# Expert rows streamed from HBM: earlier banks, a choice cut into pieces, scores two groups behind, single rows at the end

## The chip, the cores and the metric

The kernel runs on one core of one Trainium2 chip. The metric is the device time of one execution in microseconds (us), lower is better; three executions of the kernel before gave 1175.29, 1179.24 and 1180.07 us.

## The reference, cut to what matters

Two transformer blocks work on 256 tokens of 1024 features. The first has two recurrent mixers and a gated feed-forward layer. The second has retention, stick-breaking attention, an output projection and at its end PEER, a mixture over 16384 experts of one neuron each. For each token and each of 8 heads, PEER scores two lists of 128 sub-keys, takes the 16 best of each list, adds all 16 x 16 pairs, takes the 16 best pairs, and so has 128 experts per token. It then reads a row of `expert_down` and one of `expert_up` for each:

```
top_s, top_i = lax.top_k(sub_scores, K)
cand_s = top_s[:, :, 0, :, None] + top_s[:, :, 1, None, :]
best_s, best_c = lax.top_k(cand_s.reshape(T, PEER_HEADS, K * K), K)
gate = jax.nn.softmax(best_s, axis=-1)
a = jnp.einsum('pd,ped->pe', xb, expert_down[ib])
act = jax.nn.gelu(a, approximate=False) * gb
y = jnp.einsum('pe,ped->pd', act, expert_up[ib])
```

Here K is 16, and the last three lines run for 128 tokens at a time.

## The kernel before, in words

All of it is one program with an instruction order written by hand for each engine; engines meet through counting semaphores. Up to the last 700 us it multiplies with weights that stream through a ring of slots (16 in `ring_sb`, 6 in `whi`, 4 in `x_rows`).

PEER works on **columns**. Column `col` (0 to 255) is one chosen expert for each of 128 tokens; columns 0 to 127 belong to tokens 0 to 127 (tile 0), the rest to tile 1. Head h of a tile is choice n = 8 * tile + h and gives columns 16n to 16n + 15. For each column:

- POOL issues one indirect DMA (L2062) that gathers 128 rows of 8 KB, 1 MB in all, into a row buffer. It needs the expert numbers of the choice (`VTI`) and a free buffer.
- DVE takes the dot product of the first half of each row with its token (L2006).
- For a group of columns (`GR`) ACT then takes the Gelu (L1353), DVE multiplies by the gates (L2011), and ACT makes a diagonal matrix for each column (L1358).
- PE multiplies the second half of the rows with the diagonal (L905 and L908, in `add_rows`) and adds it up in PSUM. After that the buffer is free.

There are 16 row buffers of 8 KB in the end, but at first only 7: the others still hold query weights `w_q`. POOL takes buffers from a first-in, first-out list (`free`). When PE has used the weights of head h, their buffer enters the list, at the place that `after` gives: behind column 3 for head 0, 7 for head 1, 11 for head 2, 19 for head 3, 27, 43, 59 and 75 for heads 4 to 7. So column 7 uses the buffer of column 0, column 10 that of column 3, column 11 that of head 0, column 16 that of head 1, column 21 that of head 2, and column 26 that of column 16.

Around the columns the same engines still do this. PE computes queries by head (`query_tile` for one tile, L846, for heads 0 to 2; `query_half` for both tiles, L860, from head 3 on), then ACT copies the query, PE computes the scores of the two lists (`scores`, L872), ACT copies them. DVE makes a choice n (`choose`: two lists, the pairs, the decoding into expert numbers, the gates). The dicts `second_at`, `query_at` and `choose_at` say at which group i of the main loop each runs. Choices 0 and 1 run before the loop. Tile 1 also needs its part of the output projection (`second_out`), its residual (`second_gate`, `second_add` at L1908), the sums of squares (`second_sums`, L925), the root (`n3_root`, L1290 and L1292) and the norm (`second_norm`, `shifted`).

Functions of ACT need tables: Gelu one, Exp and Ln others; a change of table is an ACT_TABLE_LOAD.

In front of PEER stands the output projection of tile 0 (`out_half`, L810). Each pair of its output blocks has a PSUM bank of a ring of four, and `bank()` makes PE wait until the bank's last reader is done. All four waits stand ahead of the first product:

```
outs = [bank((VN, ("wo2", 2 * i + 1, 0))) for i in range(4)]
```

The bank used second is read last by the gate's product at L1875 on DVE. Then follow the norm of tile 0, the queries and scores of heads 0 and 1, choice 0, and the first gather.

## Time and profile before

| what | value |
|---|---|
| executions | 1175.29, 1179.24, 1180.07 us, median 1179.24 |
| profiled execution | 1178.07 us, its span 1176.3 us |
| PE busy | 1030.6 us (88%), 5156 matmuls |
| DVE busy | 855.7 us (73%) |
| ACT busy | 419.9 us (36%) |
| gathers by POOL | 256, 268.45 MB, 55.3% of 16 DMA engines' span |
| HBM read | 376.61 MB |
| mean granted clock of TensorE | 0.956 |
| chain that ended last | PE 45%, DMA 31%, DVE 15%, ACT 5% |

Busy shares are averages over stages with different limits. The span begins with the first instruction; 1.8 us of the execution lie around it.

### The profile page before, as it was taken

The page shows a single profiled execution, that of the slowest core. Times are in us where ns is not written, and L with a number is a line of the kernel's source. Part 1 is how long each engine was busy: PE and PEld are TensorE (multiplying, and loading weights), DVE is VectorE, ACT ScalarE, POOL GpSimd, SP SyncE. Part 2 cuts the span into 40 slices and gives each one's busy share as a digit, 9 for nine tenths or more (in the row PEclk, how much of TensorE's full clock was granted, in tenths as well). Part 3 has the DMA queues.
Part 4 walks back from the last instruction along what each step waited for, and adds up shares of the span by engine and source line. Part 5 has one row for each costly group of instructions (what it writes and reads, how often), then busy time and mean ns, then how long its engine had stood idle before and what let it go on. Part 6 is the DMA issues. An engine that isn't in the chain of part 4 may idle for free.

```text
span 1176.3 us, 14387 instructions
## 1 busy us (share of the span) xinstructions
PE 1030.6 (88%) x5156; PEld 721.4 (61%) x5156; DVE 855.7 (73%) x1780; ACT 419.9 (36%) x833; POOL 285.8 (24%) x260
## 2 busy tenths in 40 slices
PE   6999999999999999988899998888668767887878
PEld 6988999999998876874555544333323323332433
DVE  5977689998868993384778767766786677677554
ACT  5644544445456654233223222221221222222112
POOL 0000000000000000034445543454335434443520
PEclk9999999999999999989999998898899889888998
DMA  9532449979927433479999999999999999999994
GB/s 357 204 125 90 147 180 350 354 293 322 326 89 309 139 109 124 180 284 340 364 420 422 422 421 421 422 420 421 423 422 421 422 422 419 423 421 421 422 421 183
DMA packets 67896, 378.61 MB, mean 322 GB/s; under 512 B 7537, under 2 KB 7921, under 8 KB 35057
## 3 DMA queue, kind: packets, MB, share of 16 engines
q0 software_dynamic: 36864, 268.45, 55.3%
q1 hardware_dynamic: 29808, 106.09, 25.0%
q10 hardware_dynamic: 1152, 3.15, 0.8%
q8 instruction: 42, 0.69, 0.2%
q14 instruction: 30, 0.24, 0.1%
HBM read 376.61 MB, written 1.05 MB: 321 GB/s over the span
## 4 chain that ended last, share of the span: by engine, by line
PE 45%; DMA 31%; DVE 15%; ACT 5%; issue 4%; POOL 1%; SPq 0%; DVEq 0%; ACTq 0%
DMA whi_rows<-in_peer,idsb 26%; PE pb L905 7%; PE pb L428 7%; PE pb L425 7%; PE pb L908 6%; PE pb L453 4%; DMA ring_sb<-in_peer,idsb 3%; DVE ring_lo L1417 3%; PE pb L640 2%; PE pb L810 2%; PE pb L860 1%; DVE ring_sb L2006 1%; PE pb L470 1%; PE pb L472 1%; PE pb L471 1%
## 5 line engine op out<-in xcount | busy, mean ns | idle before, releaser
L2006 DVE CUSTOM_DVE_ANT_0 ring_sb<-ring_sb,arena 128x1024 f32<-128x1024 f32 x137 | 166.9, 1225 | 106.8 <-DMA ring_sb<-in_peer,idsb 106.8
L905 PE MATMUL pb<-ring_sb,arena 128*128 128x512 f32 x274 | 154.2, 646 | 98.8 <-ACT arena L1358 98.7
L2062 POOL DMA_INDIRECT ring_sb<-in_peer,idsb x137 | 150.4, 1098 | 237.0 <-PE pb L908 210.2
L425 PE MATMUL pb<-xhi,whi 128*128 128x256 f32 x736 | 190.9, 293 | 1.1 <-ACT xhi L986 0.5
L428 PE MATMUL pb<-xlo,whi 128*128 128x256 f32 x736 | 186.3, 287 | 0.5 <-DVE xlo L1636 0.3
L2062 POOL DMA_INDIRECT arena<-in_peer,idsb x38 | 41.4, 1090 | 546.2 <-DVE idsb L1984 503.4
L1353 ACT ACTIVATE arena<-arena 128x4 f32<-128x4 f32 (+2 forms) x71 | 14.6, 205 | 400.4 <-DVE arena L2006 400.4
L1417 DVE TENSOR_TENSOR ring_lo<-ring_sb,whi 128x1024 fp32r<-128x1024 f32 x126 | 147.6, 1218 | 13.4 <-ACT whi L959 13.3
L905 PEld LDWEIGHTS pb<-ring_sb,arena 128*128 128x128 f32 x274 | 52.3, 202 | 167.9 <-issue 167.4
L908 PE MATMUL pb<-ring_sb,arena 128*128 128x512 f32 x274 | 151.0, 634 | 0.0
L425 PEld LDWEIGHTS pb<-xhi,whi 128*128 128x128 f32 x736 | 142.5, 194 | 5.4 <-issue 3.4
L428 PEld LDWEIGHTS pb<-xlo,whi 128*128 128x128 f32 x736 | 142.6, 194 | 4.5 <-issue 2.7
L959 ACT ACTIVATE whi<-ring_sb 128x1024 fp32r<-128x1024 f32 x126 | 125.4, 1047 | 12.5 <-DMA ring_sb<-in_w_down 9.0
L908 PEld LDWEIGHTS pb<-ring_sb,arena 128*128 128x128 f32 x274 | 55.9, 204 | 72.8 <-issue 72.8
L1358 ACT ACTIVATE arena<-cs,arena 128x128 f32<-128x128 f32 x256 | 82.6, 390 | 16.3 <-DVE arena L2011 15.6
L453 PE MATMUL pb<-xhi,ring_lo 128*128 128x256 f32 x546 | 78.6, 284 | 0.0
L2006 DVE CUSTOM_DVE_ANT_0 whi_rows<-whi_rows,arena 128x1024 f32<-128x1024 f32 x40 | 49.0, 1226 | 34.6 <-DMA whi_rows<-in_peer,idsb 34.6
L453 PEld LDWEIGHTS pb<-xhi,ring_lo 128*128 128x128 f32 x546 | 71.6, 193 | 0.0
L2006 DVE CUSTOM_DVE_ANT_0 arena<-arena 128x1024 f32<-128x1024 f32 x38 | 46.4, 1224 | 13.5 <-DMA arena<-in_peer,idsb 13.5
L2062 POOL DMA_INDIRECT whi_rows<-in_peer,idsb x40 | 46.6, 1165 | 38.7 <-PE pb L908 29.2
L1682 DVE SCALAR_TENSOR_TENSOR arena<-ring_sb,small,arena 128x1024 f32<-128x1024 f32 x42 | 51.9, 1278 | 0.0
L425 PE MATMUL pb<-ahi,whi 128*128 128x256 f32 x176 | 49.9, 284 | 0.0
(356 smaller groups left out, 1783.8 us busy)
## 6 DMA issues: line engine op xcount, KB each, us to landing
ring_sb<-in_ada SPq DMA_DIRECT2D x48, 512.0 KB, 5.6
ring_sb<-in_w_gu SPq DMA_DIRECT2D x44, 512.0 KB, 6.9
ring_sb<-in_w_in SPq DMA_DIRECT2D x38, 512.0 KB, 8.3
ring_sb<-in_w_down SPq DMA_DIRECT2D x22, 512.0 KB, 5.9
ring_sb<-in_w_out SPq DMA_DIRECT2D x16, 512.0 KB, 3.6
ring_sb<-in_w_q SPq DMA_DIRECT2D x8, 512.0 KB, 3.6
whi_rows<-in_w_q SPq DMA_DIRECT2D x6, 512.0 KB, 7.5
ring_sb<-in_peer,idsb POOLq DMA_INDIRECT x137, 27.7
```

Source lines behind the costliest of these rows:

```text
L425: e.matmul(o, hi_w(u)[:, c], xh(k), start=start, stop=False, skip_group_check=skip)
L428: e.matmul(o, hi_w(u)[:, c], xl(k), start=False, stop=False, skip_group_check=skip)
L453: e.matmul(o, lo_w(u)[:, kc(k)], hi_of(k), start=False, stop=False)
L640: mm = e.matmul(o, lo_w(u)[:, kc(n)], ah_of(k), start=False, stop=False, skip_group_check=True)
L905: mm = e.matmul(pb[4 + 2 * tile][:, :], dgr[col % 8], o[:, 1024:1536], start=begin, stop=end)
L908: e.matmul(pb[5 + 2 * tile][:, :], dgr[col % 8], o[:, 1536:2048], start=begin, stop=end).then_inc(*PU.up(("row", col)))
L959: e.activation(hi_w(u), slot(u), ACT.Copy).then_inc(*HI.up(u))
L1358: e.activation(dgr[col % 8], c_("ident"), ACT.Copy, scale=ae[:, col:col + 1]).then_inc(*AD.up(("dg", col)))
L1417: e.tensor_tensor(lo_w(u), slot(u), hi_w(u).bitcast(F32), SUB).then_inc(*LOV.up(u))
L1682: e.scalar_tensor_tensor(out=o, in0=slot(u), scalar=cs8[:, k:k + 1], in1=o, op0=MUL, op1=ADD).then_inc(*VM.up(("ada", n)))
L2006: e.tensor_tensor_reduce(o, o, h2t[tile], 1.0, 0.0, MUL, ADD, aa[:, col:col + 1]).then_inc(*VD.up(("dot", col)))
L2062: e.indirect_dma_start(rows_at[s], None, peer, bass.IndirectOffsetOnAxis(ap=idsb[:, col:col + 1], axis=0)).then_inc(s_row[s], 16)
```

## The change

First, the banks of the output projection are awaited one by one, in the order 0, 2, 3, 1 of the ring. Second, choice 1 is cut into pieces (`best_of_list`, `pair_up`, `best_of_pairs`, `decode`, `gates`), and the dots of columns 0 to 3 and their weights stand between the pieces. ACT runs the Exp of choice 1 behind group 1 and the root of tile 1 ahead of group 2. Third, the query of head 2, tile 0 moves behind the first group on PE. A query of the loop now stands behind `add_rows` in its group, and the scores of that query two groups later (on ACT: the copy of the query one group later and of the scores three). The `second_at` entry of head 2 moves from group 5 to 9, queries of later heads one group earlier, choices from 3 on one group later. `after` reads GR[i - 1] for GR[i - 2]: buffers of heads 0, 1, 2 enter the list behind columns 7, 11 and 31, those of heads 3 to 7 behind 19, 27, 43, 59 and 75 as before. Fourth, columns 240 to 255 are two groups of two and twelve of one, where they were two of four and eight of one.

```
-        GR = [range(0, 2), range(2, 4)] + [range(i, i + 4) for i in range(4, 248, 4)] + [range(i, i + 1) for i in range(248, 256)]
+        GR = [range(0, 2), range(2, 4)] + [range(i, i + 4) for i in range(4, 240, 4)] + [range(i, i + 2) for i in range(240, 244, 2)] + [range(i, i + 1) for i in range(244, 256)]
-        second_at = {3: 0, 4: 1, 5: 2}
-        query_at = {6: (3, 0), 7: (3, 1)} | {4 * h - 8 + j: (h, j) for h in range(4, 8) for j in range(2)}
-        choose_at = {4: 2, 8: 3} | {4 * n - 6: n for n in range(4, 16)}
+        second_at = {3: 0, 4: 1, 9: 2}
+        query_at = {5: (3, 0), 6: (3, 1)} | {4 * h - 9 + j: (h, j) for h in range(4, 8) for j in range(2)}
+        choose_at = {4: 2, 9: 3} | {4 * n - 5: n for n in range(4, 16)}
...
-            outs = [bank((VN, ("wo2", 2 * i + 1, 0))) for i in range(4)]
-            where["wo2"] = outs
+            outs = where["wo2"] = [(turn[0] + i) % 4 for i in (0, 2, 3, 1)]
+            turn[0] += 4
             for i in range(4):
+                bank((VN, ("wo2", 2 * i + 1, 0)), outs[i])
                 out_half(0, i, range(4, 8), pb[outs[i]])
...
-            query_tile(2, 0)
...
             for i in range(NB + 1):
-                if i in second_at:
-                    query_tile(second_at[i], 1)
-                if i in query_at:
-                    query_half(*query_at[i])
                 if i == 60:
                     keep_clock(10)
                 if i:
                     add_rows(i - 1)
                 if i == 1:
+                    query_tile(2, 0)
+                if i == 2:
                     second_sums()
                     scores(2, (0,))
+                if i - 2 in second_at:
+                    scores(second_at[i - 2], (1,))
+                if i - 2 in query_at and query_at[i - 2][1]:
+                    scores(query_at[i - 2][0], (0, 1))
                 if i in second_at:
-                    scores(second_at[i], (1,))
-                if i in query_at and query_at[i][1]:
-                    scores(query_at[i][0], (0, 1))
+                    query_tile(second_at[i], 1)
+                if i in query_at:
+                    query_half(*query_at[i])
...
             choose(0)
             second_gate(range(4))
-            choose(1)
-            second_gate(range(4, 8))
             for i in range(NB + 1):
-                if i - 1 in query_at and query_at[i - 1][1]:
-                    scores(query_at[i - 1][0], (0, 1))
-                if i - 1 in second_at:
-                    scores(second_at[i - 1], (1,))
+                if i == 2:
+                    n3_root(1)
                 if i < NB:
                     prepare(i)
                 if i == 0:
+                    second_gate(range(4, 8))
+                if i == 1:
+                    choose(1)
                     query_tile(2, 0)
                     second_squares()
-                if i == 1:
-                    n3_root(1)
+                if i == 2:
                     scores(2, (0,))
-                if i == 2:
                     shifted(1)
-                if i in second_at:
-                    query_tile(second_at[i], 1)
-                if i in query_at and query_at[i][1]:
-                    query(query_at[i][0])
+                if i - 3 in second_at:
+                    scores(second_at[i - 3], (1,))
+                if i - 3 in query_at and query_at[i - 3][1]:
+                    scores(query_at[i - 3][0], (0, 1))
+                if i - 1 in second_at:
+                    query_tile(second_at[i - 1], 1)
+                if i - 1 in query_at and query_at[i - 1][1]:
+                    query(query_at[i - 1][0])
...
             choose(0)
-            choose(1)
-            for i in range(NB + 1):
+            best_of_list(1, 0)
+            dot(0)
+            best_of_list(1, 1)
+            dot(1)
+            pair_up(1)
+            weigh(0)
+            best_of_pairs(1)
+            dot(2)
+            dot(3)
+            decode(1, 0, 16)
+            weigh(1)
+            second_add()
+            gates(1)
+            for i in range(2, NB + 1):
                 if i < NB:
                     prepare(i)
-                if i == 0:
-                    second_add()
...
-            after = {GR[i - 2][-1]: h for i, h in second_at.items()} | {GR[i - 2][-1]: h for i, (h, j) in query_at.items() if j}
+            after = {GR[i - 1][-1]: h for i, h in second_at.items()} | {GR[i - 1][-1]: h for i, (h, j) in query_at.items() if j}
```

## Rows read from the trace of the kernel before

**Rows 1.** Page, part 2: GB/s moved by the DMA engines, 40 slices of 29.4 us.

```profile
GB/s 357 204 125 90 147 180 350 354 293 322 326 89 309 139 109 124 180 284 340 364 420 422 422 421 421 422 420 421 423 422 421 422 422 419 423 421 421 422 421 183
```

**Rows 2.** Busy time by stretch (PE, PEld, DVE, ACT, POOL, PEclk, DMA share, GB/s).

```profile
1000.00:1010.00 10.00, 8.49 (x13) 3.66 (x14) 6.73 (x14) 2.97 (x10) 2.60 (x2) 0.63 1.01 421
...
1160.00:1165.00 5.00, 5.00 (x13) 2.23 (x12) 2.86 (x7) 1.21 (x4) 0.00 (x0) 1.00 0.06 26
```

**Rows 3.** Timeline, DVE: dots of rows 11, 26, 28 and 255 (start us, us, operation, idle, releaser).

```profile
544.08 1.23 DVE L2006 CUSTOM_DVE_ANT_0 ring_sb<-ring_sb,arena 128x1024 f32<-128x1024 f32 x1 [3.06 <-DMA ring_sb<-in_peer,idsb]
...
587.09 1.23 DVE L2006 CUSTOM_DVE_ANT_0 ring_sb<-ring_sb,arena 128x1024 f32<-128x1024 f32 x1 [3.32 <-DMA ring_sb<-in_peer,idsb]
...
592.97 1.22 DVE L2006 CUSTOM_DVE_ANT_0 x_rows<-x_rows,arena 128x1024 f32<-128x1024 f32 x1 [0.81 <-DMA x_rows<-in_peer,idsb]
...
1166.57 1.23 DVE L2006 CUSTOM_DVE_ANT_0 x_rows<-x_rows,arena 128x1024 f32<-128x1024 f32 x1 [0.80 <-DMA x_rows<-in_peer,idsb]
```

**Rows 4.** Timeline, POOL: gathers 0, 7, 11, 24 and 26 issued.

```profile
503.82 1.08 POOL L2062 DMA_INDIRECT arena<-in_peer,idsb  x1 [503.37 <-DVE idsb L1984]
...
524.42 1.20 POOL L2062 DMA_INDIRECT arena<-in_peer,idsb  x1 [10.30 <-PE pb L908]
...
538.59 0.94 POOL L2062 DMA_INDIRECT ring_sb<-in_peer,idsb  x1 [3.98 <-PE pb L846]
...
569.19 1.99 POOL L2062 DMA_INDIRECT ring_sb<-in_peer,idsb  x1 [0.30 <-issue]
...
581.48 0.94 POOL L2062 DMA_INDIRECT ring_sb<-in_peer,idsb  x1 [9.06 <-PE pb L908]
```

**Rows 5.** Timeline, PE: end of the last projection, then the second block's output projection.

```profile
470.46 0.28 PE L454 MATMUL pb<-xhi,ring_lo 128*128 128x256 f32 x1
473.01 1.24 PE L810 MATMUL pb<-xn,ring_sb 128*128 128x128 f32 x9 [2.27 <-DVE arena L1875]
```

**Rows 6.** Timeline, DVE: the second choice, and the residual addition of tile 1.

```profile
507.49 0.29 DVE L1917 MAX8 arena<-arena 128x8 f32<-128x128 f32 x1
...
511.45 0.43 DVE L1917 MAX8 arena<-arena 128x8 f32<-128x256 f32 x1
...
513.82 0.15 DVE L1949 TENSOR_SCALAR arena<-arena 128x1 f32<-128x1 f32 x1
...
516.56 0.17 DVE L1984 SCALAR_TENSOR_TENSOR idsb<-arena 128x16 uint32<-128x16 f32 x1
...
519.73 1.22 DVE L1908 TENSOR_TENSOR hT<-hT,arena 128x1024 f32<-128x1024 f32 x1
```

**Rows 7.** Timeline, PE: query tile, first row, scores of tile 1, half a query.

```profile
512.75 3.74 PE L846 MATMUL pb<-xn,ring_sb 128*128 128x128 f32 x32
...
520.39 2.05 PE L905 MATMUL pb<-arena 128*128 128x512 f32 x2 [3.91 <-ACT arena L1358]
...
573.68 1.05 PE L872 MATMUL pb<-subk_sb,sq 128*128 128x128 f32 x4 [3.41 <-ACT sq L1324]
...
586.19 3.62 PE L860 MATMUL pb<-xn,ring_sb 128*128 128x256 f32 x16
```

**Rows 8.** Timeline, ACT: root of tile 1's norm, then the table for the Gelu.

```profile
528.69 0.37 ACT L1290 ACTIVATE stdt<-pb,cs 128x128 f32<-128x128 f32 x1 [3.00 <-PE pb L925]
...
530.97 1.28 ACT L1353 ACT_TABLE_LOAD   x1
```

**Rows 9.** Timeline, PE and ACT: three groups near the end, last diagonal, last row.

```profile
1138.09 1.10 PE L905 MATMUL pb<-ring_sb,arena 128*128 128x512 f32 x2 [2.85 <-ACT arena L1358]
...
1148.05 2.04 PE L905 MATMUL pb<-ring_sb,arena 128*128 128x512 f32 x2 [2.85 <-ACT arena L1358]
...
1168.27 0.40 ACT L1358 ACTIVATE arena<-cs,arena 128x128 f32<-128x128 f32 x1 [0.23 <-DVE arena L2011]
...
1168.29 1.02 PE L905 MATMUL pb<-whi_rows,arena 128*128 128x512 f32 x2
...
1170.01 1.02 PE L905 MATMUL pb<-x_rows,arena 128*128 128x512 f32 x2
```

More of the change, by code:

```diff
@@ L1995, in choose, with dot, weigh @@
                 gates(n)
-            def prepare(i):
-                for col in GR[i]:
-                    tile = col // 128
-                    s, v = row_of[col]
-                    o = rows_at[s][:, 0:1024]
-                    e.wait_ge(s_row[s], v)
-                    if col % 128 == 0:
-                        for g in range(2):
-                            e.wait_ge(*AQ.at((("h2t", tile), g)))
-                    e.tensor_tensor_reduce(o, o, h2t[tile], 1.0, 0.0, MUL, ADD,
-                                           aa[:, col:col + 1]).then_inc(*VD.up(("dot", col)))
+            def dot(col):
+                tile = col // 128
+                s, v = row_of[col]
+                o = rows_at[s][:, 0:1024]
+                e.wait_ge(s_row[s], v)
+                if col % 128 == 0:
+                    for g in range(2):
+                        e.wait_ge(*AQ.at((("h2t", tile), g)))
+                e.tensor_tensor_reduce(o, o, h2t[tile], 1.0, 0.0, MUL, ADD, aa[:, col:col + 1]).then_inc(*VD.up(("dot", col)))
+            def weigh(i):
                 cols = slice(GR[i].start, GR[i].stop)
@@ L2011, in prepare @@
                 e.tensor_tensor(ae[:, cols], ae[:, cols], gts[:, cols], MUL).then_inc(*VD.up(("act", i)))
+            def prepare(i):
+                for col in GR[i]:
+                    dot(col)
+                weigh(i)
                 if i in choose_at:
```

48 lines of the change are left out of this document (29 added, 19 removed).

## The prediction

> **What bounds the kernel now.** I read the page's DMA lines first. From the slice at 588 us to the last but one the engines move 419 to 423 GB/s, and before that, from the first gather on, less [rows 1]. A steady stretch gives 421 GB/s [rows 2], so a gather of 1.049 MB takes 2.49 us. From there on nothing but the DMA sets the pace. What can be won is the time that the DMA lost before, and what follows the last landing.
>
> So I list when rows landed, by the dots that waited for them. Row 11 landed at 544.08, row 26 at 587.09, row 28 at 592.97, the last, 255, at 1166.57 [rows 3]. From row 28 there are 227 gathers in 573.6 us, 2.53 each: the queue is never empty again. **The end is the landing of row 28 plus a constant plus the tail.** Gather 0 is issued at 503.82, gather 7 at 524.42, gather 11 at 538.59, gather 26 at 581.48 [rows 4]. Gathers 11 and 26 met an empty queue: they landed 5.5 and 5.6 us after their issue. Row 28 would, at 2.49 us a row and 5.6 us for the first, have landed at 503.8 + 5.6 + 28 x 2.49 = 579.1; it landed 13.9 us later. That is all that better feeding can give.
>
> Near the end only a sixteenth of the rate is left (26 GB/s from 1160 on, [rows 2]) while rows still land, the last at 1166.57: one engine of the 16 is behind the others and sets the end. It has the same bytes to move after the change.
>
> **The change part by part.**
>
> Banks. PE ends the last projection at 470.74 and starts the output projection at 473.01, after 2.27 us of idling on the gate's product on DVE [rows 5]. Awaited one by one with that bank last, three pairs of blocks (5.4 us of products) go ahead of it. I take 2.2 us, and all before gather 0 is one chain, so gather 0 goes from 503.8 to 501.6. Bounds: 0 if another bank is late too, 2.27.
>
> Choice 1 in pieces. Before, DVE ran it in one, from 507.49 to 517.0, and only then the dots of rows landed long ago [rows 6]. A list costs 1.7, pairing 0.55, the pairs' best 2.5 (511.45 to 513.97), decoding 2.8 (to 516.73) [rows 6], a dot 1.15 to 1.2 [rows 3]. In the new order from 505.3: list to 507.0; dot 0 waits for row 0 (501.6 + 5.6 to 6) and ends at 508.8; list 510.5; dot 1 511.7; pairing and weights 512.5; pairs 515.1; dots 2 and 3 517.4; decoding 520.3; weights 520.5; the addition of 1.2 (519.73, [rows 6]) to 521.7. PE gets its first row at 513.1 where it was 520.39 [rows 7], a gain of 7.3; the buffers of rows 0 and 1 are free at 515 and 517. Gathers 7 and 8 now queue behind gather 6 (landing at 522 or later: 501.6 + 5.6 + 6 x 2.49), so the hole in front of 524.42 [rows 4] closes. The expert numbers of choice 1 come at 520.3 instead of 516.7; that is covered, since gather 16 needs a buffer that comes far later. If the cover were gone it would cost 3.6.
>
> What is late next is group 2, columns 4 to 7. Its dots can run from 524 on, but on ACT the root of tile 1 now stands ahead of its Gelu. Chain: weights of group 1 at 520.5, two diagonals to 521.3, a table load of 1.28 (as the one in [rows 8]), Exp to 523.1, copy and squares to 524.5. PE has added rows 2 and 3 by then (521.2 to 524.7, 1.72 each by two rows of [rows 9]; query tile 2 with its 3.74 us [rows 7] lies ahead, from 516.7 to 520.4, in a gap). Sums take 1.9, to 526.6. From the root's start to the Gelu of the group there were 532.25 - 528.69 = 3.6 us, of which a 0.4 copy is now behind [rows 8]: Gelu at 530.0, PE at row 4 at 531.0. So gather 11, which now takes row 4's buffer, is issued at 533.1 and lands at 538.7. **Gain at row 11: 5.4 us.**
>
> What the trace shows of a table load is 1.28 us of ACT [rows 8], and the change has one more of them on this chain. The Trainium skill (ScalarE: Activation LUTs, What ACT_TABLE_LOAD costs) gives 2.66 us for a switch, with the drain. That would make this sum 1.4 us worse; the chain as traced (Ln, load, Exp, copy, load, Gelu in 3.6 us) has no room for it, so the row decides.
>
> Scores two groups behind. At 573.68 PE waited 3.41 us for ACT's copy of a query, which stood behind the group's dots, and then did the scores and half a query before the rows of that group [rows 7]; gather 26 waited 9.06 us for them [rows 4], and the queue ran dry. In the new order PE takes the rows first. By 2.49 us a row from row 11: row 15 lands at 548.8, its group is weighed at 550.5, choice 2 (9.5 us as choice 1) ends at 560.2, rows 16 to 19 are ready for PE at 565.7, gather 25 is issued at 567.9 and lands at 573.5, where the queue would have it at 573.6. So this spot closes, just. Queries and scores stay on PE (3.6 us for half a query, [rows 7]) between groups and are covered while each group's period is 9.95.
>
> From row 11 to row 28 took 48.9 us; 17 gathers at 2.49 are 42.3. Of the 6.6 over, 2.1 is the hole at row 26. The other 4.5 came with the queue not empty, but shallow. I take that 2.0 of them go with a fuller queue and 2.5 stay (bounds 0 and 4.5). **Gain from 11 to 28: 4.1.**
>
> Clock. PE has nothing between 527.2 and 531.0. After 3.91 us of idling the clock was at its lower level, 1.2 GHz, for the first rows: two matmuls took 2.05 us [rows 7]. After 2.85 they took 2.04 once and 1.10 once [rows 9], and after 2.27 it stayed high [rows 5]. If it falls, rows 4 and 5 take 1.7 us longer, gather 11 with them. I put 1.3 for it.
>
> Fewer buffers. Columns 12 to 43 have one less in flight (head 0's buffer enters four columns later, head 1's too, head 2's twenty later). It costs nothing as long as the spots above close; uncovered it is 2.49 us at each.
>
> Tail. Before, the group of four at 1148.05 met half clock, and PE then had no pause until the end: the last diagonal was there at 1168.67, PE came to it at 1170.01 [rows 9]. With single columns from 244 on (1.72 of each 2.49 us) it starts on the diagonal: 1.2 us. Bounds: 0, and a loss of 1.7 if the clock is at half for the last column.
>
> Sum: 5.4 + 4.1 - 1.3 + 1.2 = 9.4 us. The profiled execution is 1178.1 (span 1176.3 and 1.8 around it), so 1168.7; the median of the runs is 1.2 above it. I say 1169.5.
>
> **The rivals.**
>
> A, the DMA's own pace. All 4.5 us stay, the clock falls, the tail gives half: 5.4 + 2.1 - 1.7 + 0.6 = 6.4, about 1172.5. For it: rows 12 to 24 came in over 2.49 each with gathers queued.
>
> B, the holes move. One buffer less makes gathers 15 and 25 late, both of which I find with no slack. Two holes of 2.49 and the clock leave 9.4 - 5.4 = 4, about 1175: no change that can be measured. Against it: rows first on PE.
>
> C, slower. Gather 11 waits for the root on ACT. If its chain is 3 us longer than I have it, gather 11 gains 2.4 and not 5.4, and each of choices 2, 3 and 4, with nine to eleven buffers in flight, then opens a hole of 4 us. Together 9.4 - 3 - 12 = -5.6: about 1184. It decides from the point where gather 25 is issued after 577.
>
> D, dots against gathers. While dots ran without a pause an issue took 1.99 us, where it took 0.94 at 538.59 [rows 4]; now dots run while gathers 3 to 6 are issued. At most 4 us on POOL, and four gathers queue ahead of them, so the time is that of the forecast, or 1 us more. The Trainium skill (SBUF — State Buffer, SBUF: two separate sides) has GpSimd locked out of writing descriptors while a DVE operation holds the port pair that both share; by it alone the first gathers come late.
>
> E, the change does more: all 4.5 go, the clock holds: 1165.
>
> **How the numbers follow.** Forecast with D 0.56, own range 1166 to 1171.5; A 0.17, B 0.16, C 0.04, E 0.07. A measurement here can tell about 0.5%, 5.9 us, from no change, so under 1173.3 is faster. Faster: 0.56 + 0.14 of A + 0.07 = 0.77; same: 0.03 of A + 0.16 = 0.19; slower 0.04. The range leaves out C, half of E and the worse half of B: 1165 to 1175.5.
>
> **What would show it.** Output projection at 470.9 and gather 0 at 501.6; PE's first row at 513; gather 7 before 517; gather 11 at 533 and its row at 539; no wait of POOL over 6 us on rows 16 to 19; row 28 at 584 to 585; the last landing 8 us earlier; PE on the last row right behind its diagonal. It is wrong if row 11 lands after 542, or if rows 11 to 28 take 48 us or more.

## The result and the profile after

The changed kernel takes 1169.01 us (median of 4 runs, 1167.22 to 1170.07), the kernel before on the same chip 1178.9 (4 runs). The ratio is 0.992, 95% interval 0.9893 to 0.9946. The profiled execution took 1169.98 us, with a span of 1168.1. It is faster by 0.8%, clear of noise, and the forecast was 1169.5. Two executions that lie far out, 2063.16 us of the kernel with a hole in mid-stream and 1691.88 us of the kernel before, both in a slow state, stand in no figure below.

The spans differ by 8.2 us. The timelines say where they went, in stretches that follow one another:

| stretch | before | after | gained |
|---|---|---|---|
| start to gather 0 issued | 503.82 | 500.48 | 3.3 |
| gather 0 to row 11 landed | 40.26 | 38.43 | 1.8 |
| row 11 to row 28 | 48.89 | 47.38 | 1.5 |
| row 28 to row 255 | 573.60 | 573.22 | 0.4 |
| row 255 to the end | 9.7 | 8.6 | 1.1 |

The page's line of the DMA rate for the kernel after, 40 slices of 29.2 us, for [rows 1]:

```profile
GB/s 358 207 126 91 148 178 358 349 291 320 325 105 289 162 108 117 191 330 341 364 423 421 421 422 421 421 422 421 421 421 421 422 422 421 422 421 422 421 421 198
```

The bound is what it was: 421 to 423 GB/s from 584 us on. The slice from 496 to 526 us moved 330 GB/s where 284 stood, the two behind it 341 and 364, where 340 and 364 stood.

The timeline of DVE after, the dots that answer to [rows 3] (rows 11, 25 to 28 and 255; columns as there):

```profile
538.91 1.23 DVE L2022 CUSTOM_DVE_ANT_0 ring_sb<-ring_sb,arena 128x1024 f32<-128x1024 f32 x1 [5.58 <-DMA ring_sb<-in_peer,idsb]
...
577.03 1.22 DVE L2022 CUSTOM_DVE_ANT_0 arena<-arena 128x1024 f32<-128x1024 f32 x1 [3.15 <-DMA arena<-in_peer,idsb]
579.84 1.23 DVE L2022 CUSTOM_DVE_ANT_0 x_rows<-x_rows,arena 128x1024 f32<-128x1024 f32 x1 [1.57 <-DMA x_rows<-in_peer,idsb]
583.09 1.23 DVE L2022 CUSTOM_DVE_ANT_0 ring_sb<-ring_sb,arena 128x1024 f32<-128x1024 f32 x1 [2.02 <-DMA ring_sb<-in_peer,idsb]
586.29 1.23 DVE L2022 CUSTOM_DVE_ANT_0 ring_sb<-ring_sb,arena 128x1024 f32<-128x1024 f32 x1 [1.54 <-DMA ring_sb<-in_peer,idsb]
...
1159.51 1.23 DVE L2022 CUSTOM_DVE_ANT_0 ring_sb<-ring_sb,arena 128x1024 f32<-128x1024 f32 x1 [0.80 <-DMA ring_sb<-in_peer,idsb]
```

Row 28 lands 6.7 us earlier than in [rows 3] and row 255 7.1. Row 25 came 4.38 us behind row 24 (572.65), where a full queue gives 2.49: there is still a hole, one row ahead of the old one.

The timeline of POOL after, gathers 0, 4, 7, 9, 11 and 25, for [rows 4]:

```profile
500.48 1.07 POOL L2094 DMA_INDIRECT arena<-in_peer,idsb  x1 [500.04 <-DVE idsb L2001]
...
506.27 1.98 POOL L2094 DMA_INDIRECT ring_sb<-in_peer,idsb  x1 [0.85 <-PE pb L810]
...
513.46 1.62 POOL L2094 DMA_INDIRECT arena<-in_peer,idsb  x1 [2.50 <-PE pb L909]
...
521.06 0.94 POOL L2094 DMA_INDIRECT x_rows<-in_peer,idsb  x1 [4.45 <-PE pb L909]
...
532.29 1.85 POOL L2094 DMA_INDIRECT ring_sb<-in_peer,idsb  x1 [8.02 <-PE pb L909]
...
571.07 1.17 POOL L2094 DMA_INDIRECT arena<-in_peer,idsb  x1 [10.07 <-PE pb L909]
```

The wait of 10.30 us in front of gather 7 is down to 2.50, as the pieces were meant to do. But POOL then waits 8.02 us in front of gather 11 and 10.07 in front of gather 25. The waits moved more than they shrank.

The timeline of PE after, for [rows 5], [rows 7] and [rows 9]: the last projection and the output projection, the first row, row 4, the rows of group 5, the last row.

```profile
469.62 0.28 PE L454 MATMUL pb<-xhi,ring_lo 128*128 128x256 f32 x1
469.74 2.51 PE L810 MATMUL pb<-xn,ring_sb 128*128 128x128 f32 x21
...
511.23 1.10 PE L906 MATMUL pb<-arena 128*128 128x512 f32 x2 [1.66 <-ACT arena L1362]
...
528.61 2.05 PE L906 MATMUL pb<-ring_sb,arena 128*128 128x512 f32 x2 [3.87 <-ACT arena L1362]
...
567.04 2.05 PE L906 MATMUL pb<-arena 128*128 128x512 f32 x2 [3.52 <-ACT arena L1362]
568.88 1.92 PE L909 MATMUL pb<-arena 128*128 128x512 f32 x2
570.58 1.92 PE L906 MATMUL pb<-x_rows,arena 128*128 128x512 f32 x2
...
1161.76 1.10 PE L906 MATMUL pb<-ring_sb,arena 128*128 128x512 f32 x2 [0.51 <-ACT arena L1362]
```

The reader is to see three things. The 2.27 us of idling in front of the output projection is gone. The first row comes at 511.23, 9.2 us earlier than in [rows 7]. And twice PE idled over 3.5 us and then worked at the lower clock, 1.2 GHz: two matmuls in 2.05 us, where at 2.4 GHz they take 1.02. The second of these falls on group 5, and gather 25 waits for the buffer of that group's first row.

The timeline of ACT after, for [rows 8], the root of tile 1 and its two table loads, then the Gelu of group 2:

```profile
524.33 0.37 ACT L1292 ACTIVATE stdt<-pb,cs 128x128 f32<-128x128 f32 x1 [1.12 <-PE pb L925]
524.71 1.28 ACT L1294 ACT_TABLE_LOAD   x1
526.00 0.31 ACT L1294 ACTIVATE rstd<-stdt 128x128 f32<-128x128 f32 x1
526.33 1.28 ACT L1357 ACT_TABLE_LOAD   x1
527.62 0.20 ACT L1357 ACTIVATE arena<-arena 128x4 f32<-128x4 f32 x1
```

Group 2's rows had been multiplied on DVE by 526; their Gelu waits for the root ahead of it. Row 4 on PE waits for the Gelu, and gather 11 for row 4's buffer.

### The profile page after: what moved, and what is told of

Read it like the earlier page. It is cut to its first block, busy times and chain, and to the rows that moved or that the text cites. A ratio compares the mean times of both kernels' runs of the same rounds, so it can differ in the third digit from the quotient of the medians.

```text
span 1168.1 us, 14405 instructions
## 1 busy us (share of the span) xinstructions
PE 1032.5 (88%) x5156; PEld 720.9 (62%) x5156; DVE 854.8 (73%) x1784; ACT 421.3 (36%) x838; POOL 290.2 (25%) x260
## 4 chain that ended last, share of the span: by engine, by line
PE 46%; DMA 30%; DVE 15%; ACT 5%; issue 4%; POOL 1%; SPq 0%; POOLq 0%; DVEq 0%; ACTq 0%
DMA xn<-in_peer,idsb 22%; PE pb L906 8%; PE pb L428 7%; PE pb L425 7%; PE pb L909 7%; DMA ring_sb<-in_peer,idsb 5%; PE pb L453 4%; DVE ring_lo L1422 3%; PE pb L640 2%; PE pb L810 2%; PE pb L861 1%; DVE ring_sb L2022 1%; DMA arena<-in_peer,idsb 1%; PE pb L470 1%; PE pb L472 1%
## 5 line engine op out<-in xcount | busy, mean ns | idle before, releaser
L906 PE MATMUL pb<-ring_sb,arena 128*128 128x512 f32 x274 | 152.1, 639 | 73.7 <-ACT arena L1362 73.7
L2094 POOL DMA_INDIRECT ring_sb<-in_peer,idsb x137 | 162.2, 1184 | 193.8 <-PE pb L909 175.7
L2022 DVE CUSTOM_DVE_ANT_0 ring_sb<-ring_sb,arena 128x1024 f32<-128x1024 f32 x137 | 164.3, 1223 | 53.5 <-DMA ring_sb<-in_peer,idsb 53.5
L2094 POOL DMA_INDIRECT arena<-in_peer,idsb x38 | 39.9, 1049 | 567.9 <-DVE idsb L2001 500.0
L1422 DVE TENSOR_TENSOR ring_lo<-ring_sb,whi 128x1024 fp32r<-128x1024 f32 x126 | 147.5, 1220 | 13.3 <-ACT whi L961 13.3
L909 PE MATMUL pb<-ring_sb,arena 128*128 128x512 f32 x274 | 148.3, 624 | 0.0
L2022 DVE CUSTOM_DVE_ANT_0 arena<-arena 128x1024 f32<-128x1024 f32 x38 | 46.5, 1224 | 31.8 <-DMA arena<-in_peer,idsb 31.8
L906 PE MATMUL pb<-arena 128*128 128x512 f32 x76 | 43.2, 652 | 27.7 <-ACT arena L1362 27.6
L2022 DVE CUSTOM_DVE_ANT_0 x_rows<-x_rows,arena 128x1024 f32<-128x1024 f32 x30 | 36.7, 1224 | 31.9 <-DMA x_rows<-in_peer,idsb 31.9
```

The source lines that it names most:

```text
L906: mm = e.matmul(pb[4 + 2 * tile][:, :], dgr[col % 8], o[:, 1024:1536], start=begin, stop=end)
L909: e.matmul(pb[5 + 2 * tile][:, :], dgr[col % 8], o[:, 1536:2048], start=begin, stop=end).then_inc(*PU.up(("row", col)))
L1422: e.tensor_tensor(lo_w(u), slot(u), hi_w(u).bitcast(F32), SUB).then_inc(*LOV.up(u))
L2022: e.tensor_tensor_reduce(o, o, h2t[tile], 1.0, 0.0, MUL, ADD, aa[:, col:col + 1]).then_inc(*VD.up(("dot", col)))
L2094: e.indirect_dma_start(rows_at[s], None, peer, bass.IndirectOffsetOnAxis(ap=idsb[:, col:col + 1], axis=0)).then_inc(s_row[s], 16)
```

## The experiments

All ratios are against the kernel before, timed on the same chip in the same rounds. The kernel after was not timed again beside them, so an experiment is compared with it by ratio (0.992, interval 0.9893 to 0.9946) and by landings counted from gather 0, one trace each. How far such landings differ by chance can be seen from the kernels before, banks alone and tail alone, which have the same order between gather 0 and row 28: there row 28 lands 89.15, 89.82 and 89.15 us behind gather 0, row 255 662.75, 662.47 and 661.76. So 1 us at row 255 says nothing, and 2 us not much.

**The banks alone** (the kernel before, with this edit):

```diff
-            outs = [bank((VN, ("wo2", 2 * i + 1, 0))) for i in range(4)]
-            where["wo2"] = outs
+            outs = where["wo2"] = [(turn[0] + i) % 4 for i in (0, 2, 3, 1)]
+            turn[0] += 4
             for i in range(4):
+                bank((VN, ("wo2", 2 * i + 1, 0)), outs[i])
```

> The kernel before with the banks awaited one by one, nothing else. Theory (everything ahead of gather 0 is one chain, and the holes behind it keep their size): gather 0 and all landings 2.3 us earlier, time 2.3 us less than the kernel before (ratio 0.998). Rival (the holes in the queue at rows 7 to 26 are tied to engines that are late for other reasons and absorb it): gather 0 is 2.3 us earlier, row 28 under 1 us earlier, no gain in time.

1174.2 us, ratio 0.997 [0.9955, 0.9985]. Gather 0 at 500.41 and the last row at 1162.88, 662.5 behind it (662.8 before): the gain before gather 0 goes through to the end whole. Of the 3.4 us in this trace 0.9 lie ahead of the edit, where this execution ran earlier (the last projection ends at 469.83, before at 470.74), so 2.5 are the banks'. The time is 3.7 us less where 2.3 was expected.

**The tail alone** (the kernel before, with the last sixteen columns as two twos and twelve singles):

> The kernel before with the last sixteen columns as two twos and twelve singles. Theory (PE's backlog after a group of four at the lower clock is what the end waited for): from the landing of row 255 to the end of the span 8.6 us instead of 9.7, time 1.1 us less (0.999). Rival (only the clock counts, and it falls at another place): PE still has no pause in the last 15 us, and the distance from last landing to end stays at 9.7.

1176.95 us, ratio 0.9993 [0.9977, 1.001], as a time not to be told from nothing. In the trace the last row lands at 1165.46 and the span ends at 1174.0, 8.5 us later, where it was 9.7 before. That is what the theory expected, and yet it does not show that the edit did it: the kernel with the banks alone and the one with rows and list alone (below) end on the old groups of columns, and there too it is 8.5 and 8.6 us. PE near the end of the kernel with the banks alone, a group of four and the last row:

```profile
1144.34 2.05 PE L906 MATMUL pb<-ring_sb,arena 128*128 128x512 f32 x2 [2.83 <-ACT arena L1359]
...
1165.12 1.10 PE L906 MATMUL pb<-x_rows,arena 128*128 128x512 f32 x2 [0.23 <-ACT arena L1359]
```

The lower clock met this group of four too, but for two pairs of matmuls (2.05 and 1.54 us) and not for four (2.04, 1.91, 1.91 and 1.43 us in the trace of before), and PE had caught up before the last row. In the kernel with rows and list alone every pair from 1136.7 us on takes 1.02 to 1.10 us. So the 9.7 us are those of one trace in three with the old groups; what the edit is worth on the average is not shown.

**No pieces** (the kernel after, with choice 1 in one stretch, the root and `query_tile(2, 0)` where they were before):

```diff
-            best_of_list(1, 0)
-            dot(0)
-            best_of_list(1, 1)
-            dot(1)
...
+            choose(1)
+            for i in range(NB + 1):
```

> The changed kernel with choice 1 in one piece ahead of the dots again, and root, query tile 2 and residual back where they were; banks, scores two behind and tail stay. Theory (the pieces are what brings gather 11 forward by some 3 us beyond the banks): the hole in front of gather 7 is back, gather 7 issued near 521, row 11 lands near 541 to 542, time 3 us over the changed kernel, about 1172. Rival (the slots of heads 0 and 1, entering the list later, are what holds gather 11): row 11 as in the changed kernel at 539, time within 1 us of it.

1169.51 us, ratio 0.9925 [0.9901, 0.9949]: the same time as the kernel after. That is the rival's figure; the theory had 1172. The timeline of POOL, gathers 6, 7 and 11:

```profile
509.49 0.94 POOL L2082 DMA_INDIRECT ring_sb<-in_peer,idsb  x1 [0.85 <-PE pb L810]
520.57 1.34 POOL L2082 DMA_INDIRECT arena<-in_peer,idsb  x1 [10.14 <-PE pb L909]
...
531.01 0.94 POOL L2082 DMA_INDIRECT ring_sb<-in_peer,idsb  x1 [2.12 <-PE pb L909]
```

The old wait in front of gather 7 is back, 10.14 us, and yet row 11 lands at 539.30, only 0.4 us later than with pieces. What both kernels have alike is PE's row 4: 528.61 with pieces, 528.78 without. It hangs on the Gelu of group 2, and for that Gelu two things are due at almost the same time. One is the root of tile 1 with its table loads, which the pieces do not shorten: with them it ends at 527.62, without them at 527.39. The other is the dot of row 7, which the pieces make earlier. Without them it comes last:

```profile
526.54 1.23 DVE L2020 CUSTOM_DVE_ANT_0 arena<-arena 128x1024 f32<-128x1024 f32 x1 [3.13 <-DMA arena<-in_peer,idsb]
527.80 0.20 ACT L1356 ACTIVATE arena<-arena 128x4 f32<-128x4 f32 x1 [0.41 <-DVE arena L2020]
```

So the pieces take away one bound and meet the other 0.2 us ahead of it. They issue gathers 7 to 10 5 to 7 us earlier; the queue works them off and then stands empty in front of gather 11. Busy time where the queue ran dry (columns as in [rows 2]), first without pieces, then with them:

```profile
520.00:523.00 3.00, 3.00 (x16) 1.91 (x15) 3.00 (x5) 1.98 (x3) 1.55 (x2) 1.00 0.32 60
```

```profile
530.00:535.00 5.00, 5.00 (x11) 2.13 (x10) 2.69 (x6) 2.68 (x7) 2.40 (x2) 0.85 0.12 30
```

An early stretch was bought with a hole of much the same size four rows later. The pieces also brought the fall of the clock at row 4: without them PE idles 1.10 us there and a pair takes 1.10 us.

**No scores** (the kernel after, with queries, scores, choices and the list of buffers where they were before; banks, pieces and tail stay):

> The changed kernel with scores, queries, choices and the entry of the buffers back where they were; banks, pieces and tail stay. Theory (scores two behind spare PE the wait for ACT's copy in front of group 5, and the hole at row 25 or 26): PE idles over 3 us for the copy of a query again, the hole at row 26 is at least as deep as before (4.5 us or more between landings) and row 28 lands 1 to 3 us later than in the changed kernel; time 1170 to 1172. Rival (fewer buffers in flight cost as much as the order gives): row 28 within 1 us, time equal to the changed kernel or below it.

1175.85 us, ratio 0.9982 [0.9968, 0.9996]. Gather 26 waits 9.07 us at 580.74, as in [rows 4], and row 28 lands at 592.58, 6.3 us later than in the kernel after. The theory had the direction, but 1 to 3 us for row 28 and 1170 to 1172 for the time: this part is worth more than it said. Banks and pieces together land row 28 91.6 us behind gather 0, the banks alone 89.8, and the time is 1.65 us above that of the banks alone in the same rounds: without the other part the pieces bring nothing and by the trace cost 1.8 us.

**Rows and list alone.** What is left of the gain is in the third part. This kernel is the one before with two edits of it:

```diff
             for i in range(NB + 1):
-                if i in second_at:
-                    query_tile(second_at[i], 1)
-                if i in query_at:
-                    query_half(*query_at[i])
                 if i == 60:
                     keep_clock(10)
                 if i:
                     add_rows(i - 1)
+                if i in second_at:
+                    query_tile(second_at[i], 1)
+                if i in query_at:
+                    query_half(*query_at[i])
...
-            after = {GR[i - 2][-1]: h for i, h in second_at.items()} | {GR[i - 2][-1]: h for i, (h, j) in query_at.items() if j}
+            after = {GR[i - 1][-1]: h for i, h in second_at.items()} | {GR[i - 1][-1]: h for i, (h, j) in query_at.items() if j}
```

> The kernel before, with two things of the change: add_rows stands ahead of the query products on TensorE, and the list of buffers follows (GR[i - 1]). Scores stay in the group of their query product, banks, pieces and tail as before. Counted from gather 0's issue, row 28 landed after 89.2 us before and after 85.8 us in the kernel after. Theory (rows first is most of the gain, the scores two groups behind the smaller part): row 28 86.5 us behind gather 0, time 1174 to 1175.5 us. Rival (TensorE's wait for ScalarE's copy of the query is the cost, so that the scores' place is what brings the gain): row 28 89 us behind gather 0, time 1177.5 us.

1172.08 us, ratio 0.995 [0.9931, 0.9969]. Row 28 lands 84.2 us behind gather 0 (89.2 before, 85.8 after), row 255 656.7 (662.8 before, 659.0 after). So by row 28 these two edits bring 5.0 us, where the whole change brings 3.3 behind gather 0. Another 1.1 comes behind row 28, but the kernels with the banks alone and the tail alone are 1.0 us shorter there too, so it can't be put down to these edits. POOL's gathers 25 and 26 show the gain; no wait is over 3 us where one of 9.06 was:

```profile
570.20 1.47 POOL L2062 DMA_INDIRECT ring_sb<-in_peer,idsb  x1 [1.25 <-PE pb L846]
574.13 0.94 POOL L2062 DMA_INDIRECT arena<-in_peer,idsb  x1 [2.45 <-PE pb L908]
```

Theory expected 86.5 and left something for the scores' new place; rival 89. Neither left room for what came.

**The old list under the new order** (the kernel after, with the line of `after` alone taken back):

> The kernel after, with the one line of the buffer list as before: a buffer that a head's query weights held enters the list one group sooner than the rows of the group ahead of that query product. Theory (the list has to follow the order in which TensorE now works): gather 11 or 12 stands in front of a buffer that only the query product behind group 2's rows frees, later than the 532.3 us at which gather 11 went out in the kernel after; row 11 lands at 541 us or later, row 28 at 588 to 592 us, and the time is 1171 to 1174 us. Rival (the entry's place in the list matters little, since gathers go out one behind another anyway): row 28 at 586 us, time 1169 us.

1203.69 us, ratio 1.0217 [1.0194, 1.024]: slower than before by 26 us, and 30 us beyond what the theory had. POOL, gathers 10, 11, 16 and 25:

```profile
522.96 1.50 POOL L2094 DMA_INDIRECT ring_sb<-in_peer,idsb  x1 [0.78 <-PE pb L909]
541.43 0.94 POOL L2094 DMA_INDIRECT ring_sb<-in_peer,idsb  x1 [16.98 <-PE pb L847]
...
563.11 0.93 POOL L2094 DMA_INDIRECT ring_sb<-in_peer,idsb  x1 [15.77 <-PE pb L847]
...
593.23 0.94 POOL L2094 DMA_INDIRECT ring_sb<-in_peer,idsb  x1 [19.09 <-PE pb L861]
```

The first hole is the one foreseen: gather 11 stands before a query product that comes behind group 2's rows. What was missed is that it comes again at nearly every head: gathers 34, 52, 69 and 86 too wait 12.7 to 13.3 us for a query product. POOL issues in the list's order, so buffers of rows that PE had already used stood free behind one that PE would use last. Rows first needs the list that follows it. The new list without rows first was not tried.

**The root behind group 2** (the kernel after, with `n3_root(1)` called behind `prepare(2)`):

```diff
-                if i == 2:
-                    n3_root(1)
                 if i < NB:
                     prepare(i)
...
                 if i == 2:
+                    n3_root(1)
                     scores(2, (0,))
```

> The changed kernel with ACT's root of tile 1 behind group 2 instead of ahead of it. Theory (gather 11 waits for the buffer of row 4, and that for the root's chain in front of the Gelu of group 2): Gelu of group 2 at 526 instead of 527.6, PE's row 4 at 527 without a fall of the clock, gather 11 issued near 529.5 instead of 532.3, row 11 lands 2.5 us earlier; row 28 then 1 to 2.5 us earlier, time 1 to 2.5 us less than the changed kernel, 1167. Rival (the hole in front of row 25 is set by choice 2 and the clock, and takes the gain back): row 11 earlier, row 28 within 0.7 us of the changed kernel.

1167.11 us, ratio 0.9916 [0.99, 0.9931]. Gather 11 goes out 30.3 us behind gather 0 (31.8 after), row 11 is there 36.7 behind it or earlier (38.4), row 28 84.7 (85.8), row 255 656.9 (659.0). PE has row 4 at 528.08 and at full clock, 1.10 us for two matmuls. The trace is what the theory expected of it, but for the Gelu, which comes at 527.10 and not at 526, since it now waits for the dot of row 7. So row 4 comes only 0.5 us earlier, and most of the gain in gather 11 is the clock. As a time the gain is not shown: the ratio lies inside the interval of the kernel after.

**The clock kept before group 5, and both** (the kernel after, with 15 products of ones that keep PE busy; the second kernel has the root behind group 2 too):

```diff
+                if i == 6:
+                    keep_clock(15)
                 if i == 60:
                     keep_clock(10)
```

> The changed kernel with 15 idle products (3.4 us) on PE in front of the rows of group 5, in the pause of 3.5 us that PE has there; nothing else. Theory (the lower clock at 567 costs 3.4 us on rows 16 and 17 and makes the hole in front of gather 25): clock high at 567, gather 25 issued near 569.3 instead of 571.1, gather 26 at 571 instead of 573.7; row 25 lands near 575.2, rows 26 and 27 follow in 2.5 to 3 us; row 28 near 583.5, time 2 to 3 us less. Rival (what holds rows 25 to 28 is the DMA after an empty queue, not the issue): row 28 under 1 us earlier.

> Both of these edits together, to see if the gains add up. Theory: row 11 lands near 536.4, row 15 near 547.5, choice 2 starts 2.5 us earlier, gather 25 near 567, row 28 near 581; time 4 to 5 us under the changed kernel, 1164.5. Rival: only the larger of the two gains is left, 1167.

The first: 1168.93 us, 0.9931 [0.9915, 0.9946], row 255 657.2 us behind gather 0. The clock is high at group 5's rows (a pair in 1.10 us at 567.73) and gather 25 goes out at 569.96, 1.1 us earlier than in the kernel after, where the theory had 1.8. Row 28 lands 1.1 us earlier and the time shows no gain where 2 to 3 us were expected, so the rival is as near as the theory.

Both: 1166.47 us, 0.9911 [0.9894, 0.9927], row 255 655.2 behind gather 0. In the trace the two gains add up (3.8 us against 2.1 and 1.9), in the time they don't: 1164.5 was expected, and 1167, the rival's figure, came. Busy time by stretch (columns as in [rows 2]), first of the kernel after, then of the one with both:

```profile
530.00:545.00 15.00, 14.58 (x56) 8.30 (x55) 5.32 (x11) 4.16 (x12) 6.53 (x6) 0.95 0.69 264
560.00:575.00 15.00, 11.48 (x30) 6.22 (x29) 12.15 (x25) 3.59 (x13) 3.15 (x3) 0.77 0.84 332
```

```profile
530.00:545.00 15.00, 12.93 (x55) 7.73 (x54) 8.58 (x14) 7.49 (x17) 8.35 (x7) 1.00 0.94 350
560.00:575.00 15.00, 15.00 (x72) 10.66 (x71) 9.91 (x19) 3.50 (x12) 4.75 (x4) 1.00 0.95 370
```

In the first stretch the DMA moved 264 GB/s without the edits and 350 with both, in the second 332 and 370, and with both the granted clock is 1.00 in either. DVE's dots of rows 25 and 28 with both edits (rows 26 to 28 come at steps of 2.50, 2.48 and 2.48 us, behind the one hole that is left):

```profile
574.75 1.23 DVE L2023 CUSTOM_DVE_ANT_0 arena<-arena 128x1024 f32<-128x1024 f32 x1 [3.06 <-DMA arena<-in_peer,idsb]
...
582.21 1.23 DVE L2023 CUSTOM_DVE_ANT_0 ring_sb<-ring_sb,arena 128x1024 f32<-128x1024 f32 x1 [0.82 <-DMA ring_sb<-in_peer,idsb]
```

From row 11 to row 28 it takes 44.5 us, what the prediction had for the change itself (44.8).

**No pieces, clock kept:**

> The kernel after with choice 1 in one stretch and the root chain where it was, and with 15 clock-keeping products ahead of group 5's rows. Theory (pieces bring nothing, and the kept clock is worth what it was in the kernel with pieces, 0 to 2.5 us): 1167 to 1169 us, group 5's rows at 1.1 us a pair and row 25 landing 1 to 2.5 us before the 577.4 us of the same kernel without the kept clock. Rival (pieces are needed once the rest is faster): 1170 us or more.

1167.36 us, ratio 0.9908 [0.9888, 0.9928]. Group 5's rows run at full clock (568.01, 1.10 us), row 25 lands at 576.43, 1.0 us before the 577.43 without the kept clock (2.3 counted from gather 0, which came 1.3 us later here), and row 255 657.1 us behind gather 0. The theory holds: again no worse than with the pieces.

**Rows, list, banks and tail, and nothing else** (the kernel before with the three edits shown above and the tail):

> The kernel before with four things of the change: rows ahead of the query products on TensorE, the list of buffers that follows them, the banks, the tail. It has no pieces, the scores stay in the group of their query product, and every head and choice stands in the group in which it stood before. From the kernel with rows and list alone, whose last row landed 656.7 us behind gather 0: gather 0 at 500.4, last row at 1157.1, span 1165.6 us, time 1166 to 1167 us. Theory (the scores two groups behind, with the queries' and choices' new groups, cost some 2.4 us in the kernel after, which lands its last row 659.0 us behind gather 0): this kernel is 2 to 3 us under the kernel after. Rival (the three parts don't add up, since rows and list gained from the later gather 0): last row 659 us or more behind gather 0, time 1169 us or more, like the kernel with choice 1 in one stretch.

1168.24 us, ratio 0.992 [0.9908, 0.9932]. Gather 0 at 500.82, the last row 657.0 us behind it, span 1166.4. By the trace the parts add up: the stream is 2.0 us shorter than in the kernel after (659.0), and 1.9 shorter than without pieces (659.0), a kernel that differs from this one only in the places of queries, scores and choices. By the times the theory is not borne out: 1168.24 against the forecast 1166 to 1167, and the interval lies inside that of the kernel after. What is shown is that these four edits give all that the whole change gives. Gathers 25 and 26:

```profile
569.07 0.94 POOL L2063 DMA_INDIRECT ring_sb<-in_peer,idsb  x1 [2.31 <-PE pb L847]
572.03 0.94 POOL L2063 DMA_INDIRECT arena<-in_peer,idsb  x1 [2.03 <-PE pb L909]
```

Two things differ here from the kernel after. Gather 25 does not wait for row 16: it takes the buffer of head 2, which the query product at L847 frees, since here that buffer enters the list behind column 15 and in the kernel after behind column 31. And PE's rows of group 5 run at full clock. PE's timeline of the same kernel, in front of the rows of group 3 and of group 5:

```profile
543.02 1.19 PE L873 MATMUL pb<-subk_sb,sq 128*128 128x128 f32 x4 [3.21 <-ACT sq L1325]
544.00 1.92 PE L906 MATMUL pb<-arena 128*128 128x512 f32 x2
...
565.06 3.73 PE L847 MATMUL pb<-xn,ring_sb 128*128 128x128 f32 x32
569.36 0.68 PE L873 MATMUL pb<-subk_sb,sq 128*128 128x128 f32 x4 [0.56 <-ACT sq L1325]
569.88 1.02 PE L906 MATMUL pb<-arena 128*128 128x512 f32 x2
```

PE idles no more than 0.56 us in front of group 5 here, and 3.52 us in the kernel after. The work between groups 4 and 5 is about as long there (a query product of 3.62 us at 559.90 and scores of 0.61, here 3.73 and 0.68); the difference is when PE comes to it. Here PE waited 3.21 us for ACT's copy of head 0's query, fell to the lower clock for group 3's rows (a pair in 1.92 us) and so is at its query product only at 565.06. So the clock is lost here too, only earlier, and so is the queue: gather 16 takes the buffer of row 8, of group 3, waits 6.73 us for it and goes out at 548.40, and the DMA falls to 154 GB/s (columns as in [rows 2]):

```profile
548.00:552.00 4.00, 4.00 (x9) 1.67 (x8) 2.12 (x7) 0.49 (x2) 2.56 (x2) 0.87 0.51 154
```

In the kernel after the queue is full there (426 GB/s) and falls to 156 GB/s from 570 to 575 us. The hole in front of gather 25 is exchanged for one in front of gather 16, of 2.5 us against 3.1 (estimates: the stretches' shortfall against 421 GB/s). How much of that is head 2's buffer and how much the scores' place was not taken apart.

**A hole in mid-stream** (the kernel after, with gather 120 held back until row 119 has been used; it settles what an empty queue costs):

```diff
                 for step in until:
                     e.wait_ge(*step)
+                if col == 120:
+                    e.wait_ge(*PU.at(("row", 119)))
```

> The changed kernel with gather 120 held until PE has used row 119, so that the queue of gathers runs empty once in the steady stretch. Nothing is left out. Theory (an empty queue costs more than its own length: the rows behind it land at 3 us and more for some rows, as rows 12 to 14 and 27 to 28 did): row 120 lands 6 us after its issue, rows 121 to 123 land 3.0 to 3.3 us apart, and the time is the length of the hole (8 to 12 us) and 1.5 to 2 us more. Rival (those intervals were ACT's, DVE's or the data's): rows 121 on at 2.49 us at once, time longer by the hole alone.

1183.52 and 1182.29 us (2 executions), ratio 1.005 [1.0027, 1.0073]. The dots of rows 119 to 123 on DVE:

```profile
816.11 1.22 DVE L2022 CUSTOM_DVE_ANT_0 whi_rows<-whi_rows,arena 128x1024 f32<-128x1024 f32 x1 [1.23 <-DMA whi_rows<-in_peer,idsb]
831.63 1.23 DVE L2022 CUSTOM_DVE_ANT_0 arena<-arena 128x1024 f32<-128x1024 f32 x1 [13.86 <-DMA arena<-in_peer,idsb]
834.31 1.23 DVE L2022 CUSTOM_DVE_ANT_0 x_rows<-x_rows,arena 128x1024 f32<-128x1024 f32 x1 [1.45 <-DMA x_rows<-in_peer,idsb]
836.79 1.23 DVE L2022 CUSTOM_DVE_ANT_0 x_rows<-x_rows,arena 128x1024 f32<-128x1024 f32 x1 [1.25 <-DMA x_rows<-in_peer,idsb]
839.28 1.23 DVE L2022 CUSTOM_DVE_ANT_0 xn<-xn,arena 128x1024 f32<-128x1024 f32 x1 [1.25 <-DMA xn<-in_peer,idsb]
```

The interval of 15.52 us is 13.0 over a full queue's 2.49. The last row lands 671.9 us behind gather 0 instead of 659.0, 12.8 later. Behind the hole the rows come at 2.68, 2.48 and 2.49 us, and not at the 3.0 to 3.3 of the theory: the rival holds. This hole cost its own length and no more. Behind it all buffers were free, so that POOL issued four more gathers within 5.0 us, before row 120 had landed; the holes at rows 11 and 25 have fewer gathers behind them, and for those this run shows nothing.

## Why the prediction was right, and where it was not

**Banks: right.** 2.2 us forecast; 2.5 by the run with the banks alone, and PE starts the output projection with no idle time at all. Gather 0 at 500.48 was 1.1 us earlier than forecast; 0.8 of it is that the execution ran earlier ahead of the edit (the last projection ended at 469.90 and not at 470.74), 0.3 is the term.

**Pieces: the step that failed.** "Gain at row 11: 5.4 us" stood as the worth of banks and pieces together. Row 11 did land at 538.91, within 0.2 us of the forecast, with gather 7 at 513.46 (before 517), PE's first row at 511.23 (forecast 513.1) and gather 11 at 532.29 (forecast 533.1). Every signpost up to row 11 was met and the cause was another: without the pieces row 11 lands at 539.30. What moved it is the banks (3.3 us with the earlier execution) and rows first with its list (1.5 us: row 11 lands 40.3 us behind gather 0 before, 38.8 with rows and list alone). The prediction itself had what it takes to see this: it wrote that gather 11 takes row 4's buffer and hangs on the root and the Gelu of group 2. It should have asked when row 4 comes without the pieces. The answer, 528.8, is what makes them worth nothing here. A smaller miss inside: 5.6 us from issue to landing came from gathers that in the kernel before went out 1.1 and 1.2 us before the row ahead of them had landed. Gather 11 of the kernel after met a queue that was empty and took 6.6.

The signposts behind row 11 were met only in part. Row 28 landed at 586.29 and not at 584 to 585, POOL waited 10.07 us for row 16's buffer where no wait over 6 was to be, and rows 11 to 28 took 47.4 us, just under the 48 that would have been the sign of being wrong.

**The root's chain: right.** Gelu at 530.0 forecast, 527.62 measured, since sums and the piece before them were done earlier; from the root to the Gelu 3.3 us against 3.6 less a copy. It ends last in this stretch, but the dot of row 7 is close behind it: with the root moved behind the group the Gelu comes at 527.10, and by the trace the stream is 2.1 us shorter, mostly since the clock stays high. Two table loads lie in these 3.29 us (524.33 to 527.62), each 1.28 us, with the work of 0.37 and 0.31 us beside them. The Trainium skill (ScalarE: Activation LUTs, What ACT_TABLE_LOAD costs) puts a switch at 2.66 us with its drain; by that alone two of them would be 5.3 us, an estimate. The trace differs: both loads and the work beside them take 3.29 us, and the row decides again.

**Rows first: right in kind, its worth underrated; the scores: no gain shown.** The prediction took "scores two groups behind" as one part with 4.1 us between rows 11 and 28, measured 1.5 (48.89 to 47.38). Taken apart, rows first with the list that follows gives 3.5 us in this stretch (48.89 to 45.4) and 5.0 from gather 0 to row 28. The new places of queries, scores and choices bring nothing on top: by the traces they cost 1.9 us (659.0 without pieces against 657.0 in the kernel that differs only by them), in the times they can't be told from nothing (ratios 0.9925 and 0.992). The kernel with rows and list alone still has the scores in their old place, and PE still waits for ACT's copy of a query (2.24 us at 545.43); it gains its 5 us all the same, since the rows of the group now stand ahead of that wait.

**"This spot closes, just": wrong.** Gather 25 was to go out at 567.9, it did at 571.07, after 10.07 us of waiting, and row 25 came 1.9 us late. Choice 2 ended 1.2 us later than forecast (561.36). Another part is the clock: the text put its one loss of clock at row 4 and did not look for a second; PE idled 3.52 us in front of group 5 and took 2.05, 1.92 and 1.92 us for pairs that take 1.02 at full clock. With products of ones in the gap gather 25 goes out 1.1 us earlier and by the trace the stream is 1.9 us shorter. The third part is the term that the text put at nothing, "Fewer buffers": it was to cost nothing as long as this spot closes, and it did not close. With head 2's buffer back behind column 15, gather 25 has no need of row 16. That was rival B's mechanism, for one hole and not for two.

**Clock at row 4: right** (1.3 us forecast; two matmuls in 2.05 and 1.57 us after 3.87 us of idling, 1.6 us lost). The fall came with the pieces.

**Tail: the number met, the cause not shown.** 1.2 was forecast, 1.1 came here and 1.2 in the tail alone, all measured from the 9.7 us of one trace of before. Two kernels with the old groups of columns end 8.5 and 8.6 us behind the last landing, as with the new ones, and the time of the tail alone is not to be told from that of before. The text took one fall of the clock in one trace, at 1148.05, for what happens each time.

**Rivals.** D cost nothing: gather 4 took 1.98 us to issue while DVE worked, but gather 7 waited for its buffer anyway. A, C and E didn't come. Of the sum of 9.4 us the span shows 8.2: 1.1 more up to row 11 (5.2 measured, 5.4 less the clock's 1.3 forecast; 0.8 of it is the drift ahead of the edits), 2.6 less from 11 to 28, 0.4 more behind row 28, 0.1 less in the tail. The medians differ by 9.9, since the profiled execution of after lies 1.0 over its median and that of before 0.8 under. The number was better than its reasons. That the forecast is met within 0.5 us is luck in good part: the pieces, the tail and the scores' new place were counted as gains and are not shown to be any, rows first with its list was counted too low, and part of what the traces show lies ahead of the edits or in the one trace of before.

**Open.** Rows 12, 13, 27 and 28 of the kernel after come at 3.13 to 3.25 us although gathers are queued, and in the kernel with both edits the same rows come at 2.46 to 2.50. Other transfers don't take the time: from 530 to 550 us all packets but 2 of 835 are those of the gathers. The deep queue behind the hole in mid-stream shows no such rows; whether a shallow one is the cause was not tried. Nor was the kernel of rows, list, banks and tail tried with the root moved and the clock kept, nor the root moved without the pieces, where they might be worth something.

## What to carry to other kernels

When a wait is removed, ask what the next buffer in the same queue waits for without the edit; if that time stands still, the queue drains early and the hole reappears a few entries later. Where one engine frees buffers and another takes them in a fixed list, put first on the engine what frees most, and change the list in the same edit: the same order with the old list cost 26 us against before. Look at how long a pair of matmuls takes behind each pause of PE: a pause of 3.5 us cost more behind it, by the lower clock, than it seemed. And before a gain is put down to an edit, look at the same figure in the kernels that don't have the edit: the tail's 1.2 us are there too.

## What the runs showed that was not expected

- A dry queue cost its own length: 13.0 us of hole moved the end by 12.8, counted from gather 0, with 2.68, 2.48, 2.49 us behind it.
- A list that is out of step with its consumer fails at nearly each head again: waits of 16.98, 15.77 and 19.09 us on POOL, and four more of 12.7 to 13.3, where one was foreseen.
- Fifteen products of ones (30 matmuls, 3.51 us) in a gap of 3.5 us kept the granted clock at 1.00 and by the trace gave 1.9 us in the stream, although they compute nothing. The time shows none of it (ratio 0.9931 against 0.992).
- From the last landing to the end there are 8.5 to 8.6 us in every kernel but the trace of before (9.7), with single columns at the end or with the old group of four; no edit here got under that.
